# Latent attention: turned masks kept as ones and zeros, multiplied into the capped probabilities on VectorE

## What is computed

```python
s_idx = jnp.where(causal[None], s_idx, -jnp.inf)
_, sel = lax.top_k(s_idx, k_top)                 # k_top = 256
valid = sel <= q_pos[None, :, None]
lg_s = jnp.einsum('bqhc,bqkc->bqhk', ql, c_sel) * scale
lg_s = lg_s + bias_of_distance(q_pos - sel)      # rel_bias[t5_bucket(...)]
lg_s = jnp.where(valid[:, :, None, :], lg_s, -jnp.inf)
p = jax.nn.softmax(jnp.concatenate([lg_m, lg_s], axis=-1), axis=-1)
out = p[..., :N_META] @ c_m + p[..., N_META:] @ c_sel
```

## Time and profile before

| | us |
|---|---|
| median of 3 runs | 3623.04 |
| the runs | 3618.47, 3628.05, 3623.04 |
| the profiled execution, its time | 3618.47 |
| its span | 3616.6 |
| stage of the latent attention in it | about 2775 to 3401 |

### The profile page before, as it was taken

The page is one execution under the profiler, slowest core; times in us unless marked ns, Lnnn a source line. Parts: engine busy times, 40 slices in busy tenths (PEclk is TensorE's granted clock), DMA queues, the critical chain, the costliest instruction groups (busy, mean ns, idle before and its releaser), DMA issues. The chain is left out here.

```text
span 3616.6 us, 43933 instructions
## 1 busy us (share of the span) xinstructions
PE 3298.2 (91%) x15840; PEld 2513.5 (69%) x15840; DVE 2015.9 (56%) x3697; ACT 1408.1 (39%) x2383; POOL 884.9 (24%) x832
## 2 busy tenths in 40 slices
PE   4999999899999998986889999997896999999798
PEld 4899888656666666875667878886774666666487
DVE  7111011357666666332389999986673455555466
ACT  5000001134444444212258999242653333333354
POOL 0111111355464460000421323334242112111000
PEclk9999999899999998998999999998997999999899
DMA  5322223665454423445211344455136234222344
GB/s 204 105 80 77 82 90 119 145 139 129 108 127 105 107 69 119 140 135 198 79 42 50 91 140 150 120 158 183 49 111 167 84 73 87 59 57 58 116 149 131
DMA packets 331914, 400.83 MB, mean 111 GB/s; under 512 B 100324, under 2 KB 249188, under 8 KB 319124
## 3 DMA queue, kind: packets, MB, share of 16 engines
q1 hardware_dynamic: 259256, 288.60, 28.3%
q10 hardware_dynamic: 67488, 78.03, 7.1%
q0 software_dynamic: 4960, 31.46, 3.2%
HBM read 265.39 MB, written 132.62 MB: 110 GB/s over the span
## 5 line engine op out<-in xcount | busy, mean ns | idle before, releaser
L2241 PE MATMUL f_pO<-f_PT,f_vv 128*128 128x512 f32 (+3 forms) x944 | 381.9, 487 | 20.6 <-ACT f_PT L2271 20.6
L2335 DVE TENSOR_REDUCE f_mxc<-f_pM 128x1 f32<-128x512 f32 (+2 forms) x448 | 239.9, 541 | 215.9 <-PE f_pM L2165 128.7
L2271 ACT ACTIVATE f_PT<-f_pS 128x512 f32<-128x512 f32 (+3 forms) x472 | 221.3, 472 | 348.7 <-PE f_pS L2204 170.8
L2340 DVE CUSTOM_DVE_ANT_0 n_junk<-n_pM,n_chosen 128x512 bf16<-128x512 f32 (+4 forms) x352 | 200.2, 571 | 273.8 <-PE n_pM L2171 148.3
L2882 DVE TENSOR_SCALAR_CACHE_REDUCE sharedI<-xI,TI 128x768 bf16<-128x768 f32 (+10 forms) x276 | 339.6, 1296 | 5.4 <-DVE TI L2888 5.2
L2688 PE MATMUL cbank<-hT_high,cw_hi 128*128 128x512 f32 x800 | 319.3, 399 | 18.9 <-DVE cw_lo L2841 6.8
L582 PE MATMUL p_bank<-hT_high,p_w_hi 128*128 128x512 f32 (+1 forms) x768 | 305.0, 397 | 31.0 <-DVE p_w_lo L705 31.0
L2271 ACT ACTIVATE n_PT<-n_pS 128x512 f32<-128x512 f32 (+4 forms) x352 | 177.4, 504 | 399.0 <-PE n_pS L2221 398.7
L2688 PE MATMUL cbank<-hT_high,cw_lo 128*128 128x512 f32 x800 | 316.1, 395 | 0.0
L2688 PE MATMUL cbank<-hT_low,cw_hi 128*128 128x512 f32 x800 | 315.9, 395 | 0.0
L2241 PE MATMUL n_pO<-n_PT,n_vv 128*128 128x512 f32 (+4 forms) x704 | 307.2, 518 | 0.0
(11 more groups left out here) (424 smaller groups left out, 7417.5 us busy)
## 6 DMA issues: line engine op xcount, KB each, us to landing
f_zz<-scratch_z ACTq DMA_DIRECT2D x128, 128.0 KB, 3.0
c_w_first<-in_w_in_dram SPq DMA_DIRECT2D x26, 512.0 KB, 4.5
cw_raw<-in_w_in_dram SPq DMA_DIRECT2D x25, 512.0 KB, 4.4
p_w_raw<-in_w_in_dram SPq DMA_DIRECT2D x22, 512.0 KB, 3.7
lent<-scratch_qkb POOLq DMA_DIRECT2D x40, 256.0 KB, 10.7
scratch_z<-p_stage ACTq DMA_DIRECT2D x32, 256.0 KB, 2.4
scratch_qk_high<-p_stage ACTq DMA_DIRECT2D x32, 256.0 KB, 2.6
scratch_qk_low<-p_stage_low ACTq DMA_DIRECT2D x32, 256.0 KB, 3.2
```

The source lines that it names most:

```text
L2241: pe.matmul(pO[:, B % 2, c0:c1], lhsT=vv[0:nk, b, kt, :], rhs=PT[0:nk, u % PR, c0:c1], start=(kt == 0 and not heads[h].local), stop=(heads ...
L2271: act.activation(PT[0:nk, u % PR, c0:c1], pS[0:nk, u % SR, c0:c1], ACT.Exp, scale=0.125).then_inc(s_ex, 1)
L2335: v.tensor_reduce(to, pM[:, n % 2, 0:wd], AX.X, ALU.max).then_inc(s_mx, 1)
L2340: v.tensor_tensor_reduce(junk[:, n % 2, 0:wd], pM[:, n % 2, 0:wd], chosen[:, at:at + wd], 1.0, 3.0 * NEG, ALU.add, ALU.max, accum_out=to). ...
```

## The change

The turned masks are kept as 1 for a chosen key and 0 for another: `mask_out` no longer copies the turned 0 and -1e30 but takes a Relu of 1 + 2e-30 x. The mask's matmul in `scores(u)` goes, with its wait for the load of the masks. A new function `masked(u)` on VectorE takes the probabilities' minimum with 3e38 and multiplies by the mask, in place in `PT`, all in one operation; the cap turns a probability that overflowed at a key that was not chosen into a finite number, so that zero times it is zero. `masked(u - 1)` stands at the head of VectorE's step u. `values(u)` waits for `s_masked` instead of `s_ex`. In this stage PVLAG becomes 3, TAIL (steps after the last unit) 11 and PR, the buffers of `PT`, 4. The first block's attention (tag `f_`) is not touched.

```diff
-    PVLAG, TAIL, SR, PR = 2, 10, 3, 3
+    PVLAG, TAIL, SR, PR = (2, 10, 3, 3) if rel is None else (3, 11, 3, 4)
...
-                    if h == 0 and kt == 0:
-                        pe.wait_ge(s_mt[j], 32)
-                    at = MASK_AT[j, kt] - mask_tile_col(j, kt)
-                    last = pe.matmul(bank, lhsT=identb[0:nk, 0:nk], rhs=mkt[0:nk, at + c0:at + QB4],
-                                     start=False, stop=True, skip_group_check=True)
...
-                pe.wait_ge(s_ex, u + 1)
+                pe.wait_ge(s_ex if rel is None else s_masked, u + 1)
...
+            def masked(u):
+                h, j, kt = sw.units[u]
+                (c0, c1), nk = sw.columns(h, j, kt), sw.keys(j, kt)
+                if h == 0 and kt == 0:
+                    v.wait_ge(s_mt[j], 32)
+                at = MASK_AT[j, kt] - mask_tile_col(j, kt)
+                v.wait_ge(s_ex, u + 1)
+                p = PT[0:nk, u % PR, c0:c1]
+                v.scalar_tensor_tensor(p, p, CAP, mkt[0:nk, at + c0:at + c1], ALU.min, ALU.mult).then_inc(s_masked, 1)
...
+                if rel is not None and 0 <= u - 1 < U:
+                    masked(u - 1)
...
-                                          source[:, 0:len(full) * P].rearrange("p (a b) -> p a b", b=P), ACT.Copy)
+                                          source[:, 0:len(full) * P].rearrange("p (a b) -> p a b", b=P), ACT.Relu,
+                                          bias=1.0, scale=-2.0 / NEG)
```

More of the change, by code:

```diff
@@ L25 @@
 NEG = -1.0e30
+CAP = 3.0e38
 class Tally:
@@ L1861, in stage_attend @@
             s_mt = [m.sem(n_(f"turned_masks_loaded{j}")) for j in range(NJ)]
+            s_masked = m.sem(n_("probabilities_masked"))
         s_rq, s_part = m.sem(n_("raw_queries_loaded")), m.sem(n_("head_split"))
@@ L2215, in scores @@
                         for z in (1, 2):
-                            pe.matmul(pS[0:nk, k, to:to + wd], lhsT=ident_r[:, 0:nk], rhs=bias[:, b, z, frm:frm + wd],
+                            last = pe.matmul(pS[0:nk, k, to:to + wd], lhsT=ident_r[:, 0:nk], rhs=bias[:, b, z, frm:frm + wd],
                                       start=False, stop=True, skip_group_check=True)
-                    if h == 0 and kt == 0:
-                        pe.wait_ge(s_mt[j], 32)
-                    at = MASK_AT[j, kt] - mask_tile_col(j, kt)
-                    last = pe.matmul(bank, lhsT=identb[0:nk, 0:nk], rhs=mkt[0:nk, at + c0:at + QB4],
-                                     start=False, stop=True, skip_group_check=True)
                 last.then_inc(s_sc, 1)
@@ L2776, in mask_out @@
                     last = act.activation(turned[:, n % 4, 0:len(full)],
-                                          source[:, 0:len(full) * P].rearrange("p (a b) -> p a b", b=P), ACT.Copy)
+                                          source[:, 0:len(full) * P].rearrange("p (a b) -> p a b", b=P), ACT.Relu,
+                                          bias=1.0, scale=-2.0 / NEG)
                 if len(full) < len(kts):
                     last = act.activation(turned[0:NMETA, n % 4, len(full)],
-                                          source[0:NMETA, len(full) * P:(len(full) + 1) * P], ACT.Copy)
+                                          source[0:NMETA, len(full) * P:(len(full) + 1) * P], ACT.Relu,
+                                          bias=1.0, scale=-2.0 / NEG)
                 last.then_inc(s_mc, 1)
```

## The result

The changed kernel takes **3590.93 us** in the median of four runs (3588.72 to 3598.58); the kernel before, in four, 3625.55 (3618.47 to 3632.57). The ratio on record is 0.9911, with a 95% interval of 0.9888 to 0.9934: **0.9% faster**. It is three times the 11 us of the forecast and in its direction. It lies inside the wide range (3576 to 3642), but outside the forecast's own (3597 to 3630). The profiled execution took 3588.72 us, 29.75 us less than that of before.

What follows compares the result with a forecast made beforehand. TensorE was taken to bound the latent attention. Heads 1 to 6 gave -4.8 us, head 0 -0.8, head 7 -4.4: -10.0 in all, 3613 on the median, rounded to 3612 us; range 3576 to 3642, the forecast's own 3597 to 3630.

Steps and rivals of the forecast that it cites:

- a removed matmul is worth its start-to-start time: TensorE in the latent attention: 44 mask matmuls a head, 0.22 us each at 512 columns, give back 8.0 us a head.
- Stops: Behind block ends VectorE's 3.8 us finish delays masks and row maxima, so TensorE stops: 4.5 us a head.
- lock: VectorE masks wait beside GpSimd's subtractions (2.2 us) and casts (0.5 us) for the next head: 2.7 us a head, all reaching TensorE.
- crowding: Behind blocks of 17 and 5 units, next bursts come before VectorE has caught up: 0.5 us added.
- the lead: How far VectorE can fall behind at the row maxima before TensorE stops, with two buffers: 1.3 us.
- Head 0: First two blocks run at the DMA's pace and gain nothing; the other two bring the head to -0.8 us.
- head 7: No next head, so no lock; last 22 units have no row maxima beside them: -4.4 us.
- B: Rival, chance 0.22: the gain arrives, stops and lock cost only 1.0 and 0.5 us a head; -51 us, 3572 us.
- A: The forecast, chance 0.50: block ends and lock eat most of the gain; 3597 to 3630 us.
- C: Rival, chance 0.20: VectorE becomes the bound, a mask taking 0.89 us; +29 us, 3652 us.
- D: Rival, chance 0.08: edit does not act, masks' DMA, casts or an unseen wait set the pace; 3620 to 3626 us.
- my own signs: Forecast wrong if mask reads 0.8 us or more, TensorE stops under 3 us a head, or its mid-stage clock leaves 1.00.

Runs made afterwards that it cites:

- the floor: Changed kernel without any mask on VectorE, the values' matmul waiting for the exponential instead: 3551.18 us, 65.9 us a head.
- the kernel with the lag alone: Kernel before with only the values' lag of three units and the fourth probabilities buffer, masks still added by TensorE: 3615.16 us, 74.55 us a head.

## Why the prediction was right in direction and short in size

**TensorE bounds the stage, and a removed matmul is worth its start-to-start time.** Right; 8.0 us a head were forecast and the floor shows 8.7. The term is 9% short. The table of blocks gives 0.9 us for the smallest block, which has one full unit and four narrow ones. 0.22 + 0.45 from the earlier trace rows makes only 0.67 of that, so it is probably the estimates for the narrow units that were too low. The 122.02 us of busy time in the earlier trace rows would have given 15 us a head and been far off; the choice against it was sound.

**A mask costs 0.69 us and 0.61 from start to start.** Right: 0.683 and 0.60. VectorE was forecast at 62.5 us of busy time a head and has 64.60. Without masks it has 40.31 (the 40.6 of the forecast was right), so the masks take 24.3 for 21.9, and the 2.9 us by which masks beside GpSimd are longer are enough for the difference. The Trainium skill, in VectorE: DVE Perf Modes, section "The TRN2 errata — SBUF-src ops pay a fixed extra latency per instruction", gives (N+151)/0.96 ns for a sum of two fp32 tensors, 691 ns at 512 columns; the trace agrees, with 683 for the median mask.

**VectorE falls behind at the block ends, and TensorE stops at the row maxima.** The mechanism is right, and so are the engine, the wait and the place: 98.1 + 20.4 us of waits for `n_mxc`, no stop worth naming at the values, and 3.9 of the 4.6 us gone without the reciprocals. The size is where the **step failed**. Stops (4.5) and lock (2.7) were to cost 7.2 us a head and cost 4.6:

| us in a head | forecast | measured |
|---|---|---|
| stops behind the blocks of 17 and 5 units, with crowding | 2.5 | 2.1 |
| stop behind the block of 9, and the lock | 1.0 + 2.7 | 2.0 |
| stop behind the block of 13 | 1.0 | 0.6 |

So the term that failed is the lock, with the sentence that all of it reaches TensorE because the lead is already used up. Its subtractions were to cost 2.2 us and cost 0.65, and nothing once the finish is short; the casts' 0.5 us has no run of its own. The masks that waited for GpSimd and the finish fell into the same lateness, which counts once. The stops by themselves were near. That the block of 5 units shows none does not speak against a stop behind each block: in the head whose first scores start at 2884.71 VectorE begins the finish of the block of 17 at 2889.61 and that of the block of 5 at 2897.95, and the block of 9 lasts from 2891.0 to 2906.4:

```profile
2889.61 0.86 DVE L2372 SCALAR_TENSOR_TENSOR n_w<-n_ez,n_pO 64x256 f32<-64x256 f32 x2
...
2897.95 0.86 DVE L2372 SCALAR_TENSOR_TENSOR n_w<-n_ez,n_pO 64x256 f32<-64x256 f32 x2
```

**The lock itself.** Right as a mechanism: masks of 1.10 to 1.53 us beside the subtractions. The Trainium skill, in SBUF — State Buffer, section "SBUF: two separate sides", has every GpSimd operation that reads SBUF exclude such an operation, so the casts too; the trace agrees: masks of 0.95 us beside casts, and four casts in 2.73 us for 2.27. Not foreseen was that GpSimd's side pays too (6.53 us for 5.13).

**Head 0 and head 7.** Head 0 was to give 0.8 us and gave 7.6. In its first two blocks, which I held to be paced by the DMA, 3.0 of it came (38.6 to 35.6 us together); the mask's load of 8.0 us had stopped TensorE and now stops VectorE for 4.7. But the kernel with the lag alone, which still adds its masks on TensorE, has these blocks in 35.7 us too, so the 3.0 need not be the edit's. That the masks' loads pace them is borne out by the floor, which waits for none and takes 23.8. The two later blocks gave 4.4 instead of 0.8, by the same mis-sized terms. Head 7 gave 5.5 for 4.4.

**The sum.** 24.1 + 7.6 + 5.5 = 37.2 us out of the stage for a forecast of 10.0, whose terms added up to 3613 and were written down as 3612. Of a steady head's 4.0 us for 0.8, 0.7 come from the removed matmuls and 2.6 from the stops and the lock. The 7 us by which the stage begins later in the profile are in no term. They bring the profiled pair nearer to the forecast, which is no merit of it, and the medians do not show them. A steady head gained five times what was forecast, and the whole three times; that the result still lies in the wide range is owed to B's place in it, not to the sum.

**The rivals.** The result, 3591, lies midway between the forecast (3612) and B (3572), outside the range of A. For B the stops and the lock were to be 1.5 us a head, for A 7.2; they are 4.6. C did not happen: its mask of 0.89 us did not come true, and the run with each mask twice shows what it takes. D falls with the waits. Of my own signs, the mask's price and the granted clock held, and the stops are over 3 us a head, the point under which I called the forecast wrong. The distance of the splits, 70.5 for 73.8, was missed. The wait before the weight load of the row maxima, some 7 us a head by the forecast, reads 12.2 in the head from 3025.04; as said above, it is no measure of what TensorE loses.

## What to carry to other kernels

When work moves from a full engine to one that has room, first measure the floor with that work left out: what comes back is then a number and not a sum of guesses. Within a step of the receiving engine put first what the full engine waits for soonest; here that gave 2 us of 70 a head with no instruction less. Delays on one engine need not add: here a lock and a long finish filled the same lead, and the lock was paid only where the finish had used it up. And before work is moved on the receiving engine, look at what stands behind it in a queue: here a load waited behind a store that the moved finish made later.

## What the hardware showed that was not expected

- The lock works in both directions. Four subtractions on GpSimd take 6.53 us beside masks for 5.13 without, four casts 2.73 (up to 3.26 in one kernel) for 2.27, and GpSimd is busy for 899.7 us where it was for 884.9, with the same instructions.
- With each mask applied twice, when TensorE was busy for 319.21 of 380 us, its granted clock was 0.94 of full speed over that stretch; in the changed kernel, busy for 369.64 us of the same stretch, it stayed at 1.00:

```profile
2860.00:3240.00 380.00, 369.64 (x1642) 243.68 (x1641) 345.58 (x899) 145.43 (x281) 68.16 (x72) 1.00 0.30 67
```

  The 0.94 is a mean of two levels. In steps of 4 us the clock stands at 1.00 for most of the time and falls for a few us to 0.50, that is from 2.4 to 1.2 GHz, as here, after TensorE had been busy for 3.37 and 2.97 us of the two steps in front:

```profile
3006.00:3010.00 4.00, 3.23 (x10) 2.52 (x10) 3.93 (x9) 1.78 (x3) 0.00 (x0) 0.50 0.13 33
```

  This may add to what the second mask costs, but the head's growth is already explained by VectorE's own time.
